# A recurrent layer's reciprocal on VectorE, replaced by an exponential on ScalarE and one Newton step

## The chip, the core and the metric

The kernel runs on one core of a Trainium2 chip. TensorE (PE) does the matrix products, VectorE (DVE) and ScalarE (ACT) the elementwise work, GpSimd (POOL) elementwise work and indirect loads, and SyncE (SP) issues most loads. The engines run side by side and wait for one another by semaphores. The metric is the device time of one execution in microseconds (us), the median of several runs.

## What is computed

One layer over 128 context and 512 latent tokens of width 1024, all in fp32. After a modulated norm come products with `w_in`, a bidirectional gated linear recurrence (the place of this change), a pooling branch, a merge, an output projection, and an expert mixer that takes more than two thirds of the time. The recurrence, cut to what matters:

```
def rglru_dir(x, wa, ba, wx, bx, lam, h0, reverse):
    r = jax.nn.sigmoid(blockdiag(xf, wa, ba))
    i = jax.nn.sigmoid(blockdiag(xf, wx, bx))
    log_a = RG_C * r * jax.nn.log_sigmoid(lam)            # RG_C = 8
    a = jnp.exp(log_a)
    bterm = jnp.sqrt(-jnp.expm1(2.0 * log_a)) * (i * xf)
    h = linear_scan(a, bterm, h0f)                        # h[t] = a[t] h[t-1] + bterm[t]

# mixer
hf, sf = rglru_dir(xr, ..., h0f, False)
hb, sb = rglru_dir(xr, ..., h0b, True)
branch_a = ((hf + hb) * jax.nn.gelu(yr)) @ w_up_rnn
```

The kernel avoids exp and expm1. With s = softplus(-lambda) and T = tanh(4 s r), the identities a = 2/(1+T) - 1 and sqrt(1 - a^2) = 2 sqrt(T)/(1+T) give both terms from one tanh, one sqrt and one reciprocal q = 1/(1+T).

## The kernel before

Activations lie transposed: 128 channels on the partitions, 640 tokens along the free dimension. A row block of 128 channels is a round; the recurrence has eight, m = 0 to 7, and each has two directions d = 0, 1. With a few columns of gap the two token groups make 644 columns.

Every 128x1024 weight block is split into a high and a low part, so that each fp32 product runs as three passes. ACT writes the high part `wHi` (`split`) once the product two places earlier is done, POOL writes the low part `wLo` by a subtraction that reads two tensors (`low_of`, L393), PE multiplies (`product`, L457), and ACT takes the result out of PSUM. The two PSUM and weight buffers alternate, so ACT must have taken out product g before PE may start g + 2.

The order on each engine is the order in which the program is written. `beside(m)` lists which products PE does in round m: xr(m+2), yr(m+1), gb(m+1) and upp(m) in rounds 1 to 5, only yr7 and gb7 in round 6, only upp6 and upp7 in round 7. Then follow the products ga2 to ga5. PE also does two small groups of gate products a round (`gates`, L543).

In round m, ACT does in this order: `sigs(m, 0)`, two sigmoids of the gate products of direction 0 (once `dir_done` says that DVE has finished direction 0 of round m - 1); the first product of `beside(m)`; `sigs(m, 1)`; Tanh for both directions (in place in `gr`); Sqrt for both (into `gs`, which signals `gates_act`); the other products' splits and evictions. All ACT instructions carry line 678. An `ACT_TABLE_LOAD` stands wherever the next function isn't in the loaded table: before Sqrt, before Gelu, and before the next Sigmoid.

In round m, DVE does: the convolution of the next round (`conv`, L1101 and L1103), one product of the pooling branch (`pooled_gate`, L1144), `direction(m, 0)`, `direction(m, 1)`, then the sum of both directions (L1155) and the product with gelu (L1158), which signals `a_ready`. `direction` is L1117 to L1136: 1 + T, the reciprocal (L1118), a = 2q - 1, i times x, the forcing term, and two scans into `hdir[d]`. `ch.step` is an instruction followed by DVE's own wait for its end; `ch.link` is one without that wait.

After round 7, ACT waits for the eighth `a_ready`, writes `aHi` (8 instructions), then splits the weights of ga5; POOL writes their low part, and only then can PE go on with ga5 and the products after it.

Of the kernel before, what the change touches and what calls it, by code (L numbers as in the profile page):

```python
# [49 lines left out]
def beside(m):  # L50

    if m == 0:
        return [("xr", 2), ("ga", 0), ("ga", 1), ("upp", 0)]
    if m < 6:
        return [("xr", m + 2), ("yr", m + 1), ("gb", m + 1), ("upp", m)]
    return [("yr", 7), ("gb", 7)] if m == 6 else [("upp", 6), ("upp", 7)]
# [87 lines left out]
def build(nc, xT, posT, cT, vecs_d, iota_d, invc_d, gw_d, pw_d, keys_d, wblk, ublk, u_tab, v_tab, ident_d, iota128_d, gel_d, gate_d, yT, st_out):  # L144
    f32, f32r, u32 = mybir.dt.float32, mybir.dt.float32r, mybir.dt.uint32
    ALU, ACT, AX = mybir.AluOpType, mybir.ActivationFunctionType, mybir.AxisListType
# [4 lines left out]
    def sb(name, shape, dt=f32):  # L151
        g = nc.sbuf_tensor(name, shape, dt)
        t = g.__enter__()
        keep.append(g)
        return t
# [5 lines left out]
    def sem(name):  # L161
        return nc.semaphore(name).__enter__()
# [19 lines left out]
    stfin = sb("stfin", [128, 2, KC])  # L182
    sp = sb("sp", [128, 16])
    sp4 = sb("sp4", [128, 16])
    spt = sb("spt", [128, 4, 16])
    halves_mark = len(keep)

# [29 lines left out]
    gr = [sb(f"gr{d}", [128, 2, WH]) for d in range(2)]  # L217
    gi = [sb(f"gi{d}", [128, 2, WH]) for d in range(2)]
    gs = [sb(f"gs{d}", [128, 2, WH]) for d in range(2)]
    gq = sb("gq", [128, W])  # L220
    hdir = [sb(f"hdir{d}", [128, W]) for d in range(2)]
# [47 lines left out]
             "head_done scm_ready exp_ready tr_done htok_ready e_ready row_free act_ready gel_ready acc_ready "  # L269
             "accT_done x3_ready y_ready y_st st_st st_ready dve_c act_c mod_ready pool_held dve_held "  # L270
             "w_hi act_held eg_ready gel_free bank_free gmm_done oh_ready sm_ready tr2_done wf_ready "
             "whi_ready wlo_ready hi_first crow_mm crow_ready crow_tr mod_read").split()
    gel_st = [sem(f"gel_st{j}") for j in range(2)]
    gate_st = [sem(f"gate_st{j}") for j in range(2)]
    gs_ld = [sem(f"gs_ld{j}") for j in range(4)]
    s = {n: sem(n) for n in names}
# [399 lines left out]
    def _(act):  # L676
        def actf(out, in_, f, **kw):
            return nc.scalar.activation(out, in_, f, **kw)  # L678
# [135 lines left out]
        def out_of(name, m):  # L814
            {"xr": xr_out, "yr": yr_out, "gb": gb_out, "ga": ga_out, "upp": upp_out}[name](m)

        def sigs(m, d):
            act.wait_ge(s["gates_done"], 2 * m + d + 1)
            if m >= 1:
                act.wait_ge(s["dir_done"], 2 * (m - 1) + d + 1)  # L820
            actf(gr[d][:, :, :], P[2][:, :, 0:WH], ACT.Sigmoid, bias=col(V_BA + d * 8 + m)).then_inc(s["act_c"], 1)
            actf(gi[d][:, :, :], P[3][:, :, 0:WH], ACT.Sigmoid, bias=col(V_BX + d * 8 + m)).then_inc(s["sig_done"], 1)
# [17 lines left out]
        for m in range(KC):  # L840
            sigs(m, 0)
            around = beside(m)
            out_of(*around[0])
            sigs(m, 1)
            act.wait_ge(s["act_c"], 1 + 4 * m + 2)
            for d in range(2):

                actf(gr[d][:, :, :], gr[d][:, :, :], ACT.Tanh, scale=sp4[:, d * 8 + m:d * 8 + m + 1]
                     ).then_inc(s["act_c"], 1)
            act.wait_ge(s["act_c"], 1 + 4 * m + 4)  # L850
            for d in range(2):
                actf(gs[d][:, :, :], gr[d][:, :, :], ACT.Sqrt).then_inc(s["gates_act"], 1)
            for name, b in around[1:]:
                out_of(name, b)
# [124 lines left out]
    def _(dve):  # L979
        V = nc.vector  # L980
        ch = Chain(dve, s["dve_c"], s["dve_held"])
# [60 lines left out]
        ch.step(V.tensor_tensor(e_, e_, z_, ALU.mult))  # L1042
        ch.step(V.tensor_scalar(z_, lam, -1.0, 0.0, ALU.mult, ALU.max))
        ch.step(V.scalar_tensor_tensor(out=sp[:, :], in0=e_, scalar=2.0, in1=z_, op0=ALU.mult, op1=ALU.add))
        V.tensor_scalar(sp4[:, :], sp[:, :], 4.0, None, ALU.mult).then_inc(s["sp_ready"], 1)
        V.tensor_tensor(pbias[:, :], vecs[:, V_PB:V_PB + 4], vecs[:, V_PS:V_PS + 4], ALU.mult)
        V.memset(px[:, :], 0.0).then_inc(s["xpp_ready"], 1)
# [61 lines left out]
        def flat(t3):  # L1109
            return t3[:, :, :].rearrange("p h n -> p (h n)")  # L1110

        def direction(m, d):
            r, i_, t_ = flat(gr[d]), flat(gi[d]), flat(gs[d])
            dve.wait_ge(s["gates_act"], 2 * m + d + 1)
            dve.wait_ge(s["conv_done"], m + 1)

            ch.step(V.tensor_scalar(gq[:, :], r, 1.0, None, ALU.add))  # L1117
            ch.step(V.reciprocal(gq[:, :], gq[:, :]))  # L1118
            ch.link(V.tensor_scalar(r, gq[:, :], 2.0, -1.0, ALU.mult, ALU.add))
            ch.link(V.tensor_tensor(i_, i_, xc[:, m % 2, :], ALU.mult))  # L1120
            ch.step(V.scalar_tensor_tensor(out=t_, in0=t_, scalar=2.0, in1=gq[:, :], op0=ALU.mult, op1=ALU.mult))
            ch.step(V.tensor_tensor(t_, t_, i_, ALU.mult))
            h = hdir[d]
            for g, (c0, c1) in enumerate(((0, TA), (TA + GAP, TA + GAP + TB))):
                init = 0.0 if g == 0 else vecs[:, V_ST + d * 8 + m:V_ST + d * 8 + m + 1]
                if d == 0:
                    o_, a_, b_ = h[:, c0:c1], r[:, c0:c1], t_[:, c0:c1]
                elif c0 == 0:
                    o_, a_, b_ = h[:, c1 - 1::-1], r[:, c1 - 1::-1], t_[:, c1 - 1::-1]
                else:  # L1130
                    o_, a_, b_ = h[:, c1 - 1:c0 - 1:-1], r[:, c1 - 1:c0 - 1:-1], t_[:, c1 - 1:c0 - 1:-1]
                last = V.tensor_tensor_scan(out=o_, data0=a_, data1=b_, initial=init, op0=ALU.mult, op1=ALU.add)
            last.then_inc(s["dir_done"], 1)
            dve.wait_ge(s["dir_done"], 2 * m + d + 1)
            e = TA - 1 if d == 0 else 0
            ins = V.tensor_copy(stfin[:, d, m:m + 1], h[:, e:e + 1])  # L1136
            if m == KC - 1 and d == 1:
                ins.then_inc(s["st_ready"], 1)
# [8 lines left out]
        for m in range(KC):  # L1147
            if m + 1 < KC:
                conv(m + 1)
            if 1 <= m < 7:  # L1150
                pooled_gate(m - 1)
            for d in range(2):
                direction(m, d)
            for (c0, c1, o) in ((0, TA, 0), (TA, T, GAP)):
                last = V.tensor_tensor(hs[:, m, c0:c1], hdir[0][:, c0 + o:c1 + o], hdir[1][:, c0 + o:c1 + o], ALU.add)  # L1155
            ch.step(last)
            evicted(dve, "yr", m)
            V.tensor_tensor(hs[:, m, :], hs[:, m, :], gy[:, m % 2, :], ALU.mult).then_inc(s["a_ready"], 1)  # L1158
# [28 lines left out]
        for m in range(KC):  # L1187
            pr = G["wo", m] % 2
            multiplied(dve, "wo", m)
            for (c0, c1, g) in ((0, TA, 0), (TA, HALF, 1), (HALF, T, 1)):  # L1190
                h = c0 // HALF
                last = V.scalar_tensor_tensor(out=x[:, m, c0:c1], in0=P[pr][:, h, c0 - h * HALF:c1 - h * HALF],
                                              scalar=mod[:, 16 + m, g:g + 1], in1=x[:, m, c0:c1],
                                              op0=ALU.mult, op1=ALU.add)
# [78 lines left out]
        for h in range(HEADS):  # L1273
            dve.wait_ge(s["S_ready"], 2 * h + 2)
            for t in range(NT):
                search((h, t), before)
                before = (h, t)
                if t == 0 and h > 0:
# [10 lines left out]
                               op0=ALU.mult, op1=ALU.add).then_inc(s["e_ready"], 1)  # L1289
# [89 lines left out]
        for k in range(KC):  # L1379
            last = V.scalar_tensor_tensor(out=x[:, k, TA:T], in0=P[k // 2][:, k % 2, :], scalar=mod[:, 40 + k, 1:2],  # L1380
                                          in1=x[:, k, TA:T], op0=ALU.mult, op1=ALU.add)
        last.then_inc(s["x3_ready"], 1)
        dve.wait_ge(s["accT_done"], 1)
        for k in range(KC):
            last = V.scalar_tensor_tensor(out=x[:, k, 0:TA], in0=P[0][:, k // 4, (k % 4) * 128:(k % 4 + 1) * 128],
                                          scalar=mod[:, 40 + k, 0:1], in1=x[:, k, 0:TA], op0=ALU.mult, op1=ALU.add)
        last.then_inc(s["x3_ready"], 1)
        inv_rms(2)
        with dve.Fori(0, KC) as k:
            V.scalar_tensor_tensor(out=hs[:, ds(k, 1), :].rearrange("p a n -> p (a n)"),  # L1390
                                   in0=x[:, ds(k, 1), :].rearrange("p a n -> p (a n)"),
                                   scalar=vecs[:, ds(k + V_FG, 1)], in1=rstd[:, :],
                                   op0=ALU.mult, op1=ALU.mult).then_inc(s["y_ready"], 1)
# [83 lines left out]
```

## Time and profile before

| | us |
|---|---|
| median of 3 runs | 2393.9 |
| lowest and highest | 2392.54, 2401.06 |
| the profiled execution | 2405.23 |
| its span in the trace | 2403.4 |
| mean granted TensorE clock | 0.967 |

Shares of the span, by engine: PE 95%, weight load 81%, DVE 70%, POOL 41%, ACT 34%. The recurrence's eight rounds lie between 156 and 397 us of the span. The chain of work that ended last is, by line, PE for 74% of the span and DVE for 6%; the reciprocal's line holds 1% of it.

To read the rows further down: a row of the timeline or of the chain has the start in us from the span's start, the duration in us, the engine and line, the operation, what is written and read, and in brackets the idle time of the engine before it and what ended that. A group with "x3" is three instructions. A row of one line gives the smallest, median and largest duration in ns. A row of the windows gives, for a stretch of time, the busy us of each engine (and its instructions), then the granted PE clock (1.00 is the full one), the DMA share and GB/s.

### The profile page before, as it was taken

How to read it: one execution, taken by the hardware profiler on the slowest of the kernel's cores; microseconds unless marked ns; L12 is line 12 of the kernel's file. 1: busy time of each engine (PE TensorE's matmuls, PEld its weight loads, DVE VectorE, ACT ScalarE, POOL GpSimd, SP SyncE). 2: the span in 40 equal slices, each digit the busy share in tenths (PEclk: the TensorE clock that was granted, in tenths of full speed). 3: DMA queues.
4: the chain of work that ended last, by engine and by line, in shares of the span. 5: the costliest groups of instructions: out<-in, count | busy, mean ns of one | idle time of the engine just before them, and what ended most of it. 6: DMA issues, size and time to landing. Idle time of an engine off the chain costs nothing.

```text
span 2403.4 us, 36139 instructions
## 1 busy us (share of the span) xinstructions
PE 2281.8 (95%) x11708; PEld 1947.9 (81%) x11708; DVE 1691.7 (70%) x3334; ACT 817.3 (34%) x1034; POOL 980.9 (41%) x578
## 2 busy tenths in 40 slices
PE   6799997999999999998999999998999999999995
PEld 2789987999999888786888888886888888888883
DVE  2549996131499999101888998997777777777775
ACT  1445553111323222222544444442222222222221
POOL 0223322222132444443222222225667666676671
PEclk9899998989799999999999999998999999999997
DMA  6412223333422444444688888877888888888881
GB/s 247 177 49 66 62 62 112 117 112 117 123 62 79 138 143 140 137 142 146 218 300 302 308 311 301 313 245 234 271 268 268 271 270 268 268 273 268 267 252 70
DMA packets 232787, 467.29 MB, mean 194 GB/s; under 512 B 115344, under 2 KB 115728, under 8 KB 231056
## 3 DMA queue, kind: packets, MB, share of 16 engines
q1 hardware_dynamic: 176416, 270.82, 36.6%
q0 software_dynamic: 36864, 134.23, 16.1%
q10 hardware_dynamic: 19440, 61.35, 6.4%
q8 instruction: 40, 0.66, 0.1%
q14 instruction: 27, 0.22, 0.0%
HBM read 402.37 MB, written 63.97 MB: 194 GB/s over the span
## 4 chain that ended last, share of the span: by engine, by line
PE 74%; issue 9%; DVE 6%; DMA 5%; POOL 3%; ACT 2%; DVEq 1%; ACTq 0%; SPq 0%; POOLq 0%
PE P L653 30%; PE P L457 19%; PE P L619 15%; POOL wLo L399 3%; PE P L642 3%; DMA rows<-in_u_tab,Eg 3%; PE P L479 3%; PE P L466 1%; PE P L543 1%; DMA gel_scratch<-gel 1%; DMA raw<-in_wblk 1%; PE P L499 1%; DVE ohA L1323 1%; DVE gq L1118 1%; DVE rows L1304 1%
## 5 line engine op out<-in xcount | busy, mean ns | idle before, releaser
L678 ACT ACTIVATE wHi<-raw 128x1024 fp32r<-128x1024 f32 x330 | 346.2, 1049 | 1354.2 <-PE P L653 509.6
L399 POOL TENSOR_TENSOR wLo<-raw,wHi 128x1024 fp32r<-128x1024 f32 x192 | 466.5, 2430 | 417.1 <-ACT wHi L678 416.9
L1366 DVE TENSOR_TENSOR wfLo<-wf,wfHi 128x512 fp32r<-128x512 f32 x128 | 313.8, 2452 | 165.4 <-ACT wfHi L678 165.4
L653 PE MATMUL P<-wfHi,wHi 128*128 128x512 f32 x1024 | 409.7, 400 | 10.2 <-DVE wfLo L1366 10.2
L619 PE MATMUL P<-hHi,wHi 128*128 128x512 f32 x1024 | 411.2, 402 | 3.7 <-DVE wLo L1311 3.2
L619 PE MATMUL P<-hHi,wLo 128*128 128x512 f32 x1024 | 406.3, 397 | 0.0
L653 PE MATMUL P<-wfHi,wLo 128*128 128x512 f32 x1024 | 404.4, 395 | 0.0
L619 PE MATMUL P<-hLo,wHi 128*128 128x512 f32 x1024 | 403.7, 394 | 0.0
L653 PE MATMUL P<-wfLo,wHi 128*128 128x512 f32 x1024 | 402.4, 393 | 0.0
L393 POOL TENSOR_TENSOR wLo<-raw,wHi 128x1024 fp32r<-128x1024 f32 (+1 forms) x76 | 182.6, 2404 | 502.4 <-ACT wHi L678 502.3
L418 POOL DMA_INDIRECT rows<-in_u_tab,Eg x128 | 134.6, 1052 | 357.4 <-DVE rows L1304 336.0
L457 PE MATMUL P<-hHi,wHi 128*128 128x320 f32 x960 | 233.3, 325 | 28.3 <-DVE hLo L986 12.7
L653 PEld LDWEIGHTS P<-wfHi,wHi 128*128 128x128 f32 x1024 | 192.9, 188 | 54.7 <-issue 10.4
L653 PEld LDWEIGHTS P<-wfHi,wLo 128*128 128x128 f32 x1024 | 192.8, 188 | 50.3
L619 PEld LDWEIGHTS P<-hHi,wHi 128*128 128x128 f32 x1024 | 193.3, 189 | 47.4 <-issue 4.5
L619 PEld LDWEIGHTS P<-hHi,wLo 128*128 128x128 f32 x1024 | 192.6, 188 | 46.9
L653 PEld LDWEIGHTS P<-wfLo,wHi 128*128 128x128 f32 x1024 | 192.8, 188 | 46.0
L619 PEld LDWEIGHTS P<-hLo,wHi 128*128 128x128 f32 x1024 | 193.1, 189 | 44.8
L457 PE MATMUL P<-hLo,wHi 128*128 128x320 f32 x960 | 223.7, 315 | 0.0
L457 PE MATMUL P<-hHi,wLo 128*128 128x320 f32 x960 | 222.7, 314 | 0.0
L457 PEld LDWEIGHTS P<-hHi,wHi 128*128 128x128 f32 x960 | 165.9, 194 | 33.7 <-issue 12.5
L1323 DVE TENSOR_SCALAR ohA<-iota,keysel,SC 128x128 f32<-128x128 f32 x512 | 178.2, 349 | 0.0
(172 smaller groups left out, 3264.2 us busy)
## 6 DMA issues: line engine op xcount, KB each, us to landing
raw<-in_ublk SPq DMA_DIRECT2D x128, 512.0 KB, 3.7
raw<-in_v_tab SPq DMA_DIRECT2D x128, 512.0 KB, 3.8
raw<-in_wblk SPq DMA_DIRECT2D x116, 512.0 KB, 3.7
gel_scratch<-gel ACTq DMA_DIRECT2D x128, 256.0 KB, 2.0
gsr<-gel_scratch SPq DMA_DIRECT2D x128, 256.0 KB, 6.2
gate_scratch<-stage ACTq DMA_DIRECT2D x6, 4096.0 KB, 17.0
gsr<-gate_scratch SPq DMA_DIRECT2D x128, 192.0 KB, 5.2
x<-in_xT SPq DMA_DIRECT2D x1, 2560.0 KB, 12.3
```

Of the source, the lines that this page charges most:

```text
L393: pool.tensor_tensor(wLo[:, g % 2, 0:kk], raw[:, r, 0:kk], wHi[:, g % 2, 0:kk].bitcast(f32), ALU.subtract).then_inc(raw_used[r], 1)
L399: pool.tensor_tensor(wLo[:, j % 2, :], raw[:, j, :], wHi[:, j % 2, :].bitcast(f32), ALU.subtract).then_inc(raw_used[j], 1)
L418: pool.indirect_dma_start(out=rows[:, j % UR, :], out_offset=None, in_=tab, in_offset=bass.IndirectOffsetOnAxis(ap=Eg[:, g, j:j + 1], axis ...
L457: last = nc.tensor.matmul(P[g % 2][:, h, 0:HALF], w_[:, g % 2, k * 128:(k + 1) * 128], cols(x_, k, h), start=(st and a == 0 and b == 0), s ...
L466: last = nc.tensor.matmul(P[2][:, h, 0:HALF], ones[:, :], sq[:, k % 2, h * HALF:(h + 1) * HALF], start=(k == 0), stop=(k == KC - 1))
L479: last = nc.tensor.matmul(P[3][:, MODB(m), MODC + m * 2:MODC + m * 2 + 2], raw[:, n % RAW, k * 128:(k + 1) * 128], cvec[:, 2 * k:2 * k + 2 ...
L619: last = nc.tensor.matmul(P[0][:, j % 2, :], w_[:, j % 2, k * 128:(k + 1) * 128], x_[:, k, TA:T], start=(k == 0 and a == 0 and b == 0), st ...
L642: last = nc.tensor.matmul(P[1][:, q, n * 128:(n + 1) * 128], ohB[:, q, n, :], ohA[:, q, n, :], start=True, stop=True)
L653: last = nc.tensor.matmul(P[k // 2][:, k % 2, :], w_[:, j % 2, k * 128:(k + 1) * 128], x_[:, j % 2, :], start=(first and a == 0 and b == 0 ...
L678: return nc.scalar.activation(out, in_, f, **kw)
L1323: last = V.tensor_scalar(ohA[:, q, n, :], iota128[:, :], keysel[:, 0:1, ds(c, 1)].rearrange("p a n -> p (a n)"), SC[:, ds(c, 1)], ALU.is_e ...
L1366: V.tensor_tensor(wfLo[:, j % 2, :], wf[:, j % 2, :], wfHi[:, j % 2, :].bitcast(f32), ALU.subtract).then_inc(s["wlo_ready"], 1)
```

## The change

The reciprocal q = 1/(1+T) goes. Since (1 + exp(-8 s r)) / 2 is the same number, ACT now computes exp(-8 s r) for both directions into `hdir[d]` (free at that time, since the scans write it later), from the r that Tanh then overwrites. DVE forms q0 from it and refines it by one Newton step. ACT has a new wait ahead of the exponentials: `a_ready` of the round before, since DVE still reads `hdir` until then. The Tanh pair waits for the end of both exponentials, `exp_done`. A vector `sp8` of scales is computed once.

```
@@ sp8 = sb("sp8", [128, 16]) is allocated; semaphore exp_done is added @@
             sigs(m, 1)
             act.wait_ge(s["act_c"], 1 + 4 * m + 2)
+            if m:
+                act.wait_ge(s["a_ready"], m)
+            for d in range(2):
+                actf(hdir[d][:, :], gr[d][:, :, :].rearrange("p h n -> p (h n)"), ACT.Exp,
+                     scale=sp8[:, d * 8 + m:d * 8 + m + 1]).then_inc(s["exp_done"], 1)
+            act.wait_ge(s["exp_done"], 2 * m + 2)
             for d in range(2):
                 actf(gr[d][:, :, :], gr[d][:, :, :], ACT.Tanh, scale=sp4[:, d * 8 + m:d * 8 + m + 1]
...
+        V.tensor_scalar(sp8[:, :], sp[:, :], -8.0, None, ALU.mult)
         V.tensor_scalar(sp4[:, :], sp[:, :], 4.0, None, ALU.mult).then_inc(s["sp_ready"], 1)
...
-            ch.step(V.tensor_scalar(gq[:, :], r, 1.0, None, ALU.add))
-            ch.step(V.reciprocal(gq[:, :], gq[:, :]))
-            ch.link(V.tensor_scalar(r, gq[:, :], 2.0, -1.0, ALU.mult, ALU.add))
+            ch.step(V.tensor_scalar(gq[:, :], hdir[d][:, :], 0.5, 0.5, ALU.mult, ALU.add))
+            ch.step(V.scalar_tensor_tensor(out=r, in0=r, scalar=1.0, in1=gq[:, :], op0=ALU.add, op1=ALU.mult))
+            ch.step(V.scalar_tensor_tensor(out=gq[:, :], in0=r, scalar=-2.0, in1=gq[:, :], op0=ALU.add, op1=ALU.mult))
+            ch.link(V.tensor_scalar(r, gq[:, :], -2.0, -1.0, ALU.mult, ALU.add))
             ch.link(V.tensor_tensor(i_, i_, xc[:, m % 2, :], ALU.mult))
-            ch.step(V.scalar_tensor_tensor(out=t_, in0=t_, scalar=2.0, in1=gq[:, :], op0=ALU.mult, op1=ALU.mult))
+            ch.step(V.scalar_tensor_tensor(out=t_, in0=t_, scalar=-2.0, in1=gq[:, :], op0=ALU.mult, op1=ALU.mult))
```

What stands on ACT in a round doesn't show in the diff alone. This is round 7 in the program before, from the sigmoids of direction 1 (into `gr` and `gi`) to the square roots (into `gs`):

```order
210 L678 ACTIVATE gr<-P,vecs 128x644 [waits dir_done,gates_done]
211 L678 ACTIVATE gi<-P,vecs 128x644
212 L678 ACTIVATE gr<-gr,sp 128x644 [waits act_c]
213 L678 ACTIVATE gr<-gr,sp 128x644
214 L678 ACT_TABLE_LOAD
215 L678 ACTIVATE gs<-gr 128x644 [waits act_c]
216 L678 ACTIVATE gs<-gr 128x644
```

The same stretch in the changed program:

```order
231 L679 ACTIVATE gr<-P,vecs 128x644 [waits dir_done,gates_done]
232 L679 ACTIVATE gi<-P,vecs 128x644
233 L679 ACT_TABLE_LOAD [waits a_ready]
234 L679 ACTIVATE hdir<-gr,sp 128x644 [waits act_c]
235 L679 ACTIVATE hdir<-gr,sp 128x644
236 L679 ACTIVATE gr<-gr,sp 128x644 [waits exp_done]
237 L679 ACTIVATE gr<-gr,sp 128x644
238 L679 ACT_TABLE_LOAD
239 L679 ACTIVATE gs<-gr 128x644 [waits act_c]
240 L679 ACTIVATE gs<-gr 128x644
```

A table load and two exponentials (`hdir<-gr,sp`) now stand between the sigmoids and the Tanh pair, with the wait for `a_ready` ahead of the load. Tanh follows Exp without a load of its own. Every round has this; no other instruction changes its place.

## Rows read from the trace of the kernel before

**Rows 1.** The page's first part: busy us, share of span, instructions of PE.

```profile
PE 2281.8 (95%) x11708; PEld 1947.9 (81%) x11708; DVE 1691.7 (70%) x3334; ACT 817.3 (34%) x1034; POOL 980.9 (41%) x578
```

**Rows 2.** Windows; columns: PE, weight load, DVE, ACT, POOL, clock, DMA, GB/s.

```profile
230.00:260.00 30.00, 30.00 (x193) 28.69 (x192) 28.95 (x27) 17.19 (x23) 9.67 (x5) 1.00 0.19 62
380.00:410.00 30.00, 19.00 (x132) 18.92 (x131) 23.89 (x29) 8.53 (x13) 7.90 (x3) 0.79 0.50 185
```

**Rows 3.** The chain that ended last, in order of time: start, us, what.

```profile
303.91 2.17 PE P L543 x8
...
332.89 2.17 PE P L543 x8
...
397.73 4.48 ACT aHi L678 x7
402.21 0.96 ACT wHi L678
403.23 4.41 POOL wLo L393
407.69 8.69 PE P L457 x48
```

**Rows 4.** Single lines of DVE: durations in ns, smallest, median, largest.

```profile
L1118 DVE RECIPROCAL gq<-gq x16: 4177/4178/4179, 176.0 to 386.5; 128x644 f32<-128x644 f32 x16
```

```profile
L1103 DVE SCALAR_TENSOR_TENSOR xc<-xrp,vecs,xc x24: 887/890/2923, 151.3 to 346.0; 128x644 f32<-128x644 f32 x24
```

**Rows 5.** Timeline of DVE, rounds 5 to 7.

```profile
320.34 0.50 DVE L1117 TENSOR_SCALAR gq<-gr 128x644 f32<-128x644 f32 x1 [0.56 <-ACT gs L678]
...
334.42 2.45 DVE L1119 TENSOR_SCALAR gr<-gq 128x644 f32<-128x644 f32 x1
...
341.87 0.83 DVE L1158 TENSOR_TENSOR hs<-hs,gy 128x640 f32<-128x640 f32 x1
...
351.17 0.50 DVE L1117 TENSOR_SCALAR gq<-gr 128x644 f32<-128x644 f32 x1 [3.55 <-ACT gs L678]
351.70 4.18 DVE L1118 RECIPROCAL gq<-gq 128x644 f32<-128x644 f32 x1
...
357.07 0.82 DVE L1121 SCALAR_TENSOR_TENSOR gs<-gs,gq 128x644 f32<-128x644 f32 x1
...
360.50 0.49 DVE L1117 TENSOR_SCALAR gq<-gr 128x644 f32<-128x644 f32 x1
...
370.74 0.82 DVE L1158 TENSOR_TENSOR hs<-hs,gy 128x640 f32<-128x640 f32 x1
374.82 0.50 DVE L1117 TENSOR_SCALAR gq<-gr 128x644 f32<-128x644 f32 x1 [3.26 <-ACT gs L678]
...
379.57 1.96 DVE L1119 TENSOR_SCALAR gr<-gq 128x644 f32<-128x644 f32 x1
...
396.23 0.82 DVE L1158 TENSOR_TENSOR hs<-hs,gy 128x640 f32<-128x640 f32 x1
```

**Rows 6.** Timeline of POOL, rounds 5 to 7.

```profile
323.14 1.29 POOL L393 TENSOR_TENSOR wLo<-raw,wHi 128x512 fp32r<-128x512 f32 x1 [5.70 <-ACT wHi L678]
...
334.12 2.39 POOL L393 TENSOR_TENSOR wLo<-raw,wHi 128x1024 fp32r<-128x1024 f32 x1 [1.11 <-ACT wHi L678]
...
362.99 2.34 POOL L393 TENSOR_TENSOR wLo<-raw,wHi 128x1024 fp32r<-128x1024 f32 x1 [9.35 <-ACT wHi L678]
376.45 4.73 POOL L393 TENSOR_TENSOR wLo<-raw,wHi 128x1024 fp32r<-128x1024 f32 x2 [11.12 <-ACT wHi L678]
```

**Rows 7.** Timeline of ACT, rounds 5 to 7.

```profile
300.49 1.06 ACT L678 ACTIVATE wHi<-raw 128x1024 fp32r<-128x1024 f32 x1 [4.39 <-PE P L457]
...
342.84 1.28 ACT L678 ACT_TABLE_LOAD   x1
...
370.50 0.79 ACT L678 ACTIVATE gi<-P,vecs 128x644 f32<-128x644 f32 x1
371.19 1.55 ACT L678 ACTIVATE gr<-gr,sp 128x644 f32<-128x644 f32 x2
372.75 1.28 ACT L678 ACT_TABLE_LOAD   x1
```

More of the change, by code:

```diff
@@ L184, in build @@
     sp4 = sb("sp4", [128, 16])
+    sp8 = sb("sp8", [128, 16])
     spt = sb("spt", [128, 4, 16])
@@ L271, in build @@
              "w_hi act_held eg_ready gel_free bank_free gmm_done oh_ready sm_ready tr2_done wf_ready "
-             "whi_ready wlo_ready hi_first crow_mm crow_ready crow_tr mod_read").split()
+             "whi_ready wlo_ready exp_done hi_first crow_mm crow_ready crow_tr mod_read").split()
     gel_st = [sem(f"gel_st{j}") for j in range(2)]
```

## The prediction

> **What bounds the kernel now.** I read the page's engine shares first: PE is busy for 95% of the span [rows 1], so only what makes PE wait can matter. Then the windows over the recurrence: in 230 to 260 us PE is busy for all 30.00 us, and DVE for 28.95 [rows 2]. The chain in order of time confirms that the rounds run at PE's pace: the gate products of two successive rounds start at 303.91 and 332.89, so a round is 28.98 us [rows 3]. DVE is nearly as full, but the chain doesn't run through it there. From round 6 on PE has few products left and the chain changes engines: in 380 to 410 us PE works only 19.00 of 30 us, at a granted clock of 0.79 [rows 2]. There the end of DVE's round 7 (396.23 + 0.82 = 397.05 us, [rows 5]) releases ACT's `aHi`, then a `wHi`, then POOL's `wLo`, and PE goes on at 407.69 [rows 3]. Everything later hangs on that instant, and nothing in it is changed. So the question is: when does the eighth `a_ready` come, 397.05 us before, and do rounds 1 to 5 stay at PE's pace?
>
> **What goes on DVE.** 16 reciprocals of 4.18 us [rows 4], each with 0.03 us until the next instruction (351.17 + 0.50 to 351.70, [rows 5]): 4.21 us. In comes, per direction, two operations of the form of L1121, 0.82 us plus 0.03 [rows 5]: 1.70 us. The two scalar operations around them stay, only their numbers and inputs change. So a direction falls by 2.5 us, from 9.33 (351.17 to 360.50, [rows 5]) to 6.83, and DVE has 16 x 2.5 = 40 us less work. In rounds 0 to 5 that is worth nothing, since PE sets the pace; what can shorten the end are the directions of rounds 6 and 7.
>
> **What comes on ACT.** No Exp is in these rows; the nearest row is the Tanh pair, same shape and same kind of scale: 1.55 us [rows 7]. Its bounds are that pair's cost and, from below, half of it should the instructions overlap entirely; I take 1.55, since it is the same engine over the same 644 columns. The order of the changed program has one table load more a round, 1.28 us [rows 7]. It starts when the second sigmoid is done (370.50 + 0.79 = 371.29, whereas Tanh started at 371.19): 0.1 us. With 0.05 us for the wait on `exp_done`, Tanh comes 0.1 + 1.28 + 1.55 + 0.05 = 3.0 us later in every round, and so does the DVE work that waits for it.
> The load's price by the row: Tanh runs from 371.19 for 1.55, the load starts at 372.75, at once, and takes 1.28. The Trainium skill ("ScalarE: Activation LUTs", What ACT_TABLE_LOAD costs) gives about 2.66 us for every switch, a drain of about 1380 ns included. The trace does not agree that a drain comes on top, so I leave it out; what it would do stands among the rivals.
>
> **The new wait.** ACT's load now waits for `a_ready` of the round before. Behind it are Exp, Tanh, Sqrt, the split for upp, the evictions of yr and gb and two more splits; PE waits for those evictions and, through POOL, for those splits. In rounds 1 to 5 they have cover: ACT is idle for 4.39 us before its `wHi` at 300.49 [rows 7], and 3.0 us later they still fit, with 1.4 us over. In rounds 6 and 7 they have none.
>
> **What the reciprocal covered.** POOL writes four `wLo` a round, three of about 2.4 us and one of 1.29 [rows 6]. The reciprocal isn't disturbed by them: 4177 to 4179 ns in all 16 [rows 4]. Other DVE operations are: L1119 takes 2.45 us at 334.42 beside POOL's 334.12, and 0.50 elsewhere, so it lost 1.95; L1103 takes up to 2923 ns against 890, so 2.03 [rows 4 to 6]. A short `wLo` should then cost 1.29 - (2.40 - 2.03) = 0.92. The new operations read two tensors, as L1103 does, so the `wLo` that lay under a reciprocal now hit. Bounds for one hit: 0 (if this form with a constant scalar is exempt) and the whole `wLo`, 2.4 or 1.29. I take 2.03 and 0.92, the measured ones.
> "SBUF — State Buffer" of the Trainium skill (SBUF: two separate sides) says that the ports shared by DVE and GpSimd are an exclusive lock, also for a DVE operation with two SBUF inputs against a GpSimd operation that reads SBUF. By that rule the exempt case is excluded; L1103's 2923 ns agrees with it, no row shows L1121's form beside POOL.
>
> **The sum, step by step.**
> 1. Round 5. Before: 320.34 to 342.70, 22.35 us, 1.95 of it a hit. New start 320.34 + 3.0 = 323.34. Length 22.35 - 1.95 - 5.0 = 15.4, plus hits of 0.92 + 2.03 + 2.03 from the three `wLo` in it, plus about 1.0 from one that starts near the end (at 343, for upp6): `a_ready` at 344.7, 2.0 later.
> 2. ACT's table load for Gelu at 342.84 [rows 7] has to wait for exactly that count: it moves to 344.7, 1.8 later. With it move the sigmoids of (6,1), and then come the 3.0: direction (6,0) starts at 351.17 + 4.8 = 356.0.
> 3. Direction (6,0) has the short `wLo` of upp7 in it, 0.92: (6,1) starts at 356.0 + 6.83 + 0.92 = 363.7, against 360.50. The split of ga2 waits for the sigmoids behind (6,0), so POOL's 362.99 [rows 6] moves along and falls into (6,1): 2.03. Before, 360.50 to 371.56 (end of L1158) were 11.06; now 11.06 - 2.5 + 2.03 = 10.6: `a_ready` at 374.3, 2.8 later.
> 4. Load 1.28, Exp 1.55, waits 0.1: Tanh at 377.25. From Tanh to DVE's start it was 374.82 - 371.19 = 3.63: (7,0) starts at 380.9, 6.1 later.
> 5. From there to the end it was 397.05 - 374.82 = 22.23, with 1.96 - 0.50 = 1.46 of a hit (L1119 at 379.57). New: 22.23 - 1.46 - 5.0 = 15.8, plus 2 x 2.03 for the two `wLo` of 376.45 that move along: 19.8. End: 400.7.
> That is 3.7 us later than 397.05. The rest of the chain is unchanged and shifts with it. PE would be idle for about 15 instead of 11 us before 407.69; the clock there is down already. `sp8` is one operation of 16 columns in a stretch where DVE has waits: nothing.
> The profiled execution's own 2405.23 us (span 2403.4) would become 2408.9. It lies 11.3 us above the median of the runs; the sum moves both alike: 2393.9 + 3.7 = 2397.6.
>
> **Rivals.**
> A. The new operations don't collide with POOL. Then round 5 ends before 342.7, (6,0) starts at 354.2, `a_ready` comes 13.66 + 1.74 later at 369.6, Tanh at 372.5, (7,0) at 376.2, the end at 392.0: 5.0 us earlier, 2388.9. For it: no row shows the form beside POOL. Against: the TENSOR_SCALAR and L1103 rows.
> B. The round becomes a loop through the new wait, longer than PE's. From `a_ready` to the next round's DVE start are 2.9 (load, Exp, wait) + 3.63 = 6.5 us; from there to `a_ready` 15.4 plus hits. Without hits 21.9 us; with four hits at the measured price, 3 x 2.03 + 0.92 = 7.0, it is 28.9, and PE's round is 28.98. That is the point from which it decides. I hold the rounds for covered because one of the four starts about when the convolution does, where DVE has some 2 us of room beside ACT's 6.5; so 26.9. If each hit costs the whole `wLo` and all four count, 3 x 2.4 + 1.29 = 8.5, the round is 30.4: 1.4 us more in each of rounds 1 to 6, so 8.6, and 3.7 at the end: 12.3 us, 2406.2. This is slower, and by just over 0.5%.
> C. The added table load costs more than its 1.28 us, say a second 1.28: 7.0 + 21.9 + 1.3 = 30.2 a round, 1.2 us x 6 = 7.3, and 2 x 1.28 + 3.7 at the end: 13.6, 2407.5. The row of the load at 372.75 speaks against it. That is the switch of the Trainium skill's page named above, which would make it 1.38 instead.
> D. DVE's saved time comes out whole, because the rounds hang on DVE after all (28.95 busy of 30): 16 x 2.5 = 40 us, 2354. PE's 30.00 of 30 speaks against it.
>
> **How the numbers follow.** The forecast gets 0.56, A 0.20, B 0.15, C 0.05, D 0.04. Faster by over 0.5% (12 us, about what a measurement of this kernel can tell from no change): D, 0.04. Slower by over 0.5%: B and C are at that edge; 0.18 with a little of the forecast's own spread. Within: 0.78. The range goes from A, 2388.9, to B, 2406.2, and a little further on both sides, since the three runs before lie 8.5 us apart: 2387 to 2408.
>
> **What would show it.** Right: no reciprocal, 16 directions of about 6.8 us where no `wLo` falls; one load more a round on ACT, at 1.28 us; gate products of successive rounds still 28.98 us apart up to round 6, PE busy for 30 of 30; operations of L1126 to L1133 with a largest duration near 2.8 us; first DVE work of round 7 near 381 and PE's ga5 near 411 us. Wrong: all those operations at 0.82 (A), rounds of over 29.5 us with PE idle before upp (B), a gap beside the loads (C), or a round much shorter than 28.98 (D).

## The result and the profile after

The changed kernel takes 2408.18 us (median of 20 runs, 2399.23 to 2416.59), the kernel before 2397.72 us over the 20 runs that were set against it. The ratio is 1.0038, 95% interval 1.0028 to 1.0049: slower by 9 us, 7 to 12. Against that stood a forecast of 3.7 us more. The stated range, 2387 to 2408 us, ends just where 2408.18 lies; counted from the forecast's own starting value, 2393.9 x 1.0038 = 2403.0 is inside it.

The profiled execution of the changed kernel happens to be one of its fastest, 2401.24 us with a span of 2399.4. Spans of single executions say little here; what holds is the position of events inside the recurrence, and the counts in long stretches.

The chain that ended last, changed kernel, in order of time (start, us, what):

```profile
303.12 2.17 PE P L544 x8
...
312.32 2.18 PE P L544 x8
316.03 1.28 ACT L679
317.33 1.57 ACT hdir L679 x2
318.92 1.56 ACT gr L679 x2
...
406.40 4.41 POOL wLo L394
410.86 9.40 PE P L458 x48
```

Up to round 5 PE still sets the pace: the gate products of rounds 4 and 5 start at 274.15 and 303.12, 28.97 us apart, against 28.98 in [rows 3]. Then the chain leaves PE one round earlier than before, through the new exponentials. ga5 starts at 410.86 instead of 407.69, in both kernels 10.64 us after the end of the eighth `a_ready`.

DVE's timeline in rounds 4 to 7 of the changed kernel (compare [rows 5]; the first row is the fifth `a_ready`):

```profile
313.19 0.83 DVE L1167 TENSOR_TENSOR hs<-hs,gy 128x640 f32<-128x640 f32 x1
...
330.38 2.43 DVE L1125 TENSOR_SCALAR gq<-hdir 128x644 f32<-128x644 f32 x1
...
333.71 2.92 DVE L1127 SCALAR_TENSOR_TENSOR gq<-gr,gq 128x644 f32<-128x644 f32 x1
...
342.15 1.89 DVE L1167 TENSOR_TENSOR hs<-hs,gy 128x640 f32<-128x640 f32 x1
...
355.46 0.50 DVE L1125 TENSOR_SCALAR gq<-hdir 128x644 f32<-128x644 f32 x1 [7.38 <-ACT gs L679]
...
356.86 1.77 DVE L1127 SCALAR_TENSOR_TENSOR gq<-gr,gq 128x644 f32<-128x644 f32 x1
...
363.25 0.50 DVE L1125 TENSOR_SCALAR gq<-hdir 128x644 f32<-128x644 f32 x1
...
366.65 2.97 DVE L1130 SCALAR_TENSOR_TENSOR gs<-gs,gq 128x644 f32<-128x644 f32 x1
...
373.15 0.82 DVE L1167 TENSOR_TENSOR hs<-hs,gy 128x640 f32<-128x640 f32 x1
380.58 0.50 DVE L1125 TENSOR_SCALAR gq<-hdir 128x644 f32<-128x644 f32 x1 [6.61 <-ACT gs L679]
...
382.84 2.52 DVE L1128 TENSOR_SCALAR gr<-gq 128x644 f32<-128x644 f32 x1
385.29 3.00 DVE L1129 TENSOR_TENSOR gi<-gi,xc 128x644 f32<-128x644 f32 x1
...
399.39 0.83 DVE L1167 TENSOR_TENSOR hs<-hs,gy 128x640 f32<-128x640 f32 x1
```

The fifth `a_ready` ends at 314.02, and the load that needs it starts at 316.03, right behind a sigmoid: 2.0 us to spare. From round 6 on there is nothing to spare.

The undisturbed direction is (7,1): 391.64 to 398.47, 6.83 us. All the others of rounds 5 to 7 hold an operation of 1.8 to 3.0 us, where a `wLo` of POOL hits. And ahead of (6,0) and (7,0) DVE waits for ACT, 7.38 and 6.61 us instead of 3.55 and 3.26 [rows 5].

What ACT does in that time, rounds 6 and 7 of the changed kernel (compare [rows 7]):

```profile
344.12 1.28 ACT L679 ACT_TABLE_LOAD   x1 [2.10 <-DVE hs L1167]
...
372.92 0.79 ACT L679 ACTIVATE gi<-P,vecs 128x644 f32<-128x644 f32 x1
374.05 1.28 ACT L679 ACT_TABLE_LOAD   x1 [0.34 <-DVE hs L1167]
375.35 1.56 ACT L679 ACTIVATE hdir<-gr,sp 128x644 f32<-128x644 f32 x2
376.94 1.56 ACT L679 ACTIVATE gr<-gr,sp 128x644 f32<-128x644 f32 x2
378.52 1.28 ACT L679 ACT_TABLE_LOAD   x1
```

The load at 344.12 waits for the sixth `a_ready`, as step 2 of the sum said; the one at 374.05 waits 0.34 us for the seventh. POOL's low parts in the same rounds start at these times (compare [rows 6]):

```profile
356.66 1.28 POOL L394 TENSOR_TENSOR wLo<-raw,wHi 128x512 fp32r<-128x512 f32 x1 [13.30 <-ACT wHi L679]
366.01 2.93 POOL L394 TENSOR_TENSOR wLo<-raw,wHi 128x1024 fp32r<-128x1024 f32 x1 [8.07 <-ACT wHi L679]
382.21 5.39 POOL L394 TENSOR_TENSOR wLo<-raw,wHi 128x1024 fp32r<-128x1024 f32 x2 [13.27 <-ACT wHi L679]
```

Each lies beside one of the long DVE operations above. So inside the recurrence nearly everything went as forecast: the eighth `a_ready` at 400.22, 3.2 us after 397.05, and 4.0 if one allows for this execution being 0.8 us ahead at round 5 (303.12 against 303.91). PE's waits moved, however. Ahead of ga5 it waits 6.57 us, where the forecast said about 15 and the kernel before has 11.00; ahead of the gate products of round 7 it waits 8.84 instead of 5.02, and 2.42 more ahead of a product at 385.06. Together that is 17.8 us instead of 16.0.

What the forecast lacks is 5 us that this stretch doesn't hold.

The windows show where they are. Two stretches that the change doesn't touch, the first in the expert scores, the second in the expert values (L619 and L653; PE busy, then its instructions in brackets), first in the kernel before:

```profile
860.00:1100.00 240.00, 239.59 (x1027) 192.48 (x1026) 106.78 (x343) 65.02 (x85) 107.04 (x43) 1.00 0.44 139
1700.00:2300.00 600.00, 600.00 (x2573) 482.67 (x2572) 465.16 (x429) 169.86 (x216) 417.05 (x241) 1.00 0.87 269
```

then in the changed kernel:

```profile
860.00:1100.00 240.00, 239.66 (x1024) 192.39 (x1023) 105.25 (x335) 65.88 (x86) 104.75 (x43) 1.00 0.43 140
1700.00:2300.00 600.00, 600.00 (x2563) 482.36 (x2562) 463.00 (x426) 169.07 (x214) 415.49 (x241) 1.00 0.86 269
```

At full granted clock and with PE busy throughout, the changed kernel does 1024 matmuls where there were 1027, and 2563 where there were 2573. A matmul takes 234.4 instead of 233.7 ns in the scores and 234.1 instead of 233.2 in the values; over 3072 matmuls in each stage that is 2.1 + 2.8 = 4.9 us. The length of the values' stage shows it too. From its first matmul to its last it takes 717.9 to 719.2 us in the six traces without the 64-byte tile `sp8`, and 721.5 to 722.3 in the eight traces with it (the kernels of the next section included). The length of the scores' stage, 861 to 871 us with the work between, varies too much to show it.

### The profile page after: what moved, and what is told of

Its sections match the earlier page's. It is cut to its first block, busy times and chain, and to the rows that moved or that the text cites. A ratio compares the mean times of both kernels' runs of the same rounds, so it can differ in the third digit from the quotient of the medians.

```text
span 2399.4 us, 36187 instructions
## 1 busy us (share of the span) xinstructions
PE 2281.2 (95%) x11708; PEld 1945.3 (81%) x11708; DVE 1675.9 (70%) x3351; ACT 839.9 (35%) x1058; POOL 983.0 (41%) x578
## 4 chain that ended last, share of the span: by engine, by line
PE 73%; issue 9%; DVE 6%; DMA 5%; POOL 3%; ACT 3%; DVEq 0%; ACTq 0%; SPq 0%; POOLq 0%
PE P L654 30%; PE P L458 17%; PE P L620 16%; POOL wLo L400 3%; PE P L643 3%; DMA gel_scratch<-gel 3%; PE P L480 2%; DMA rows<-in_u_tab,Eg 1%; PE P L467 1%; PE P L544 1%; PE P L500 1%; DMA raw<-in_wblk 1%; DVE ohA L1332 1%; DVE ohB L1330 1%; DVE rows L1313 1%
```

## The experiments

Twelve kernels ran, each beside the kernel before in five rounds, which gave 12 runs of most of them and 5 or 6 of e1, e2 and e11. The theories: **shift** (the end moves by exactly what the eighth `a_ready` moves), against **surcharge** (PE's longer waits in rounds 6 and 7 cost more later), and, once the windows were read, **placement** (the added tile makes later matmuls slower). In the table the shift is the end of the eighth `a_ready` less 397.05; "tile" is 4.9 where the kernel has the 64-byte tile `sp8`; "measured" is the ratio less one, times 2400.

| kernel | eighth a_ready | shift | shift + tile | ratio (95%) | measured, us |
|---|---|---|---|---|---|
| changed, 20 runs | 400.2 | +3.2 | +8.1 | 1.0038 (1.0028 to 1.0049) | +9.1 |
| e1 changed again | 400.2 | +3.1 | +8.0 | 1.0041 (1.0027 to 1.0055) | +9.8 |
| e2 ScalarE part | 425.9 | +28.8 | +33.7 | 1.0158 (1.0143 to 1.0174) | +37.9 |
| e3 VectorE part | 393.4 | -3.6 | +1.3 | 1.0003 (0.9990 to 1.0016) | +0.7 |
| e4 delay | 401.1 | +4.1 | +4.1 | 1.0002 (0.9989 to 1.0015) | +0.5 |
| e5 no added load | 396.4 | -0.6 | +4.3 | 1.0035 (1.0019 to 1.0050) | +8.4 |
| e6 no hits | 390.6 | -6.4 | -1.5 | 1.0007 (0.9987 to 1.0026) | +1.7 |
| e7 order, before | 395.5 | -1.6 | -1.6 | 1.0003 (0.9987 to 1.0018) | +0.7 |
| e8 order, changed | 386.9 | -10.1 | -5.2 | 0.9981 (0.9964 to 0.9998) | -4.6 |
| e9 tile alone | 397.2 | +0.2 | +5.1 | 1.0015 (0.9998 to 1.0032) | +3.6 |
| e10 changed, no tile | 400.1 | +3.1 | +3.1 | 1.0016 (1.0001 to 1.0031) | +3.8 |
| e11 order, no tile | 386.5 | -10.6 | -10.6 | 0.9940 (0.9921 to 0.9958) | -14.4 |
| e12 tile of 128 bytes | 397.3 | +0.2 | +0.2 | 0.9980 (0.9967 to 0.9992) | -4.8 |

**e1, the changed kernel again.** No edit.

> The changed kernel once more, beside the others. Shift theory (the end moves by exactly what the eighth a_ready moves, 3 to 4 us): 1.0013 to 1.0017 times the kernel before. Surcharge theory (the longer waits of PE in rounds 6 and 7 cost some 5 us more later, by a lower granted clock or late transfers): 1.003 to 1.0045. In the trace the eighth a_ready lies near 400 us under both; under the surcharge theory some later stage is longer than before by 3 us or more in this trace too.

1.0041, the eighth `a_ready` at 400.16. The excess over the shift came again: 6.7 us, where the interval allows 3.4 to 10. By the letter of the expectation the surcharge theory was the nearer one, but its cause (clock, transfers) isn't what this trace has: 1024 and 2563 matmuls in the two stretches again, at granted clock 1.00. Over all runs the mean granted clock is 0.9682 here and 0.9687 in the kernel before beside it. By the estimate made under e12 that is about 1 us.

**e2, ScalarE's part alone.** The DVE lines are those of before; Exp pair, load and wait stay.

```
-            ch.step(V.tensor_scalar(gq[:, :], hdir[d][:, :], 0.5, 0.5, ALU.mult, ALU.add))
...
+            ch.step(V.tensor_scalar(gq[:, :], r, 1.0, None, ALU.add))
+            ch.step(V.reciprocal(gq[:, :], gq[:, :]))
```

> ScalarE's part alone: Exp pair, table load, wait for a_ready; VectorE keeps the reciprocal and leaves the exponential unread. Computes the reference's result. Every round's VectorE work starts 3.0 us later with nothing given back: (6,0) near 357, (7,0) near 384, eighth a_ready near 406.3, so +9.2 us. A round's loop is 2.9 + 3.6 + 22.4 = 28.9 us, at the edge of TensorE's 28.98: if it exceeds it the rounds stretch and it is +12 us or more. If the ScalarE part did not matter: no change.

It is 38 us slower, far beyond the 9.2, and the other case named came true: the rounds stretch. The chain, from one exponential load to the next:

```profile
204.16 1.28 ACT L679
205.46 1.57 ACT hdir L679 x2
...
235.90 0.84 DVE hs L1166
236.81 1.28 ACT L679
...
266.73 0.84 DVE hs L1166
267.63 1.28 ACT L679
```

PE has left the chain. A load starts right behind DVE's `a_ready` operation, 32.65 and then 30.82 us apart, against PE's 28.98. And PE waits, in 160 to 450 us, for sigmoids, evictions and low parts that stand behind this on ACT:

```profile
PE P L544 <- ACT gi L679: 14.7, 2, 11.6
PE P L458 <- POOL wLo L394: 11.5, 2, 8.4
PE P L458 <- ACT gy L679: 10.3, 4, 3.4
```

So the loop of rival B exists. In the changed kernel the shorter directions keep it 2.0 us below PE's round (the fifth `a_ready` and the load behind it, above). The expected 28.9 us for e2's loop was too little, because it counted one hit a round. The round of the last load shown has three: a SCALAR_TENSOR_TENSOR of 3.03 us at 280.06, a scan of 2.52 instead of 0.42 at 283.99 and a TENSOR_SCALAR of 2.73 at 292.54.

**e3, VectorE's part alone.**

```
-            ch.step(V.tensor_scalar(gq[:, :], hdir[d][:, :], 0.5, 0.5, ALU.mult, ALU.add))
+            ch.step(V.tensor_scalar(gq[:, :], r, 0.5, 0.5, ALU.mult, ALU.add))
```

with the Exp pair and its waits left out.

> VectorE's part alone: the three new operations in place of the reciprocal, reading gr instead of an exponential; no Exp, no added load, no added wait. Leaves the exponential out, so the numbers of the recurrence are not the reference's. Forecast's mechanism: directions of 6.8 us plus hits of about 2.0 and 0.9 us; (6,0) still at 351, (7,0) near 372.8, eighth a_ready near 392.6, -4.4 us. If the whole VectorE saving were on the path: -40 us. If the new operations cost as much as the reciprocal once GpSimd hits them: 0.

The eighth `a_ready` came at 393.4 (392.6 expected). The whole VectorE saving of 40 us is worth 3.6 at this point. The total didn't fall by it (1.0003). With the tile's 4.9 us the sum is +1.3, inside the interval (-2.4 to 3.8); without it, -3.6 is not.

**e4, a delay.**

```
+            if m == 7:
+                for _ in range(4):
+                    ch.step(V.tensor_tensor(gq[:, :], gq[:, :], gq[:, :], ALU.mult))
```

in the kernel before, ahead of the last sum.

> The kernel before, with four extra VectorE operations (about 3.4 us together) ahead of the last sum of round 7. Nothing else changes. Shift theory: eighth a_ready +3.4 us and the total +3.4 us (1.0014). Surcharge theory by a longer idle stretch of TensorE before ga5: the total rises by clearly more, 6 us or more (1.0025 up).

`a_ready` moved by 4.1 us and the total by 0.5 (-2.6 to 3.6). This speaks against a surcharge from PE's longer idle stretch, and the shift itself lies just outside the interval. PE's wait ahead of ga5 did grow, from 11.00 to 14.41 us. So it is not shown that the end follows the eighth `a_ready` to the microsecond.

**e5, no added load.**

```
-                actf(hdir[d][:, :], gr[d][:, :, :].rearrange("p h n -> p (h n)"), ACT.Exp,
+                actf(hdir[d][:, :], gr[d][:, :, :].rearrange("p h n -> p (h n)"), ACT.Tanh,
```

> The changed kernel with Tanh in place of Exp in the added pair, so that no table load is added; the pair, its waits and VectorE's work stay. Its recurrence is not the reference's. By the price of the load as the row shows it (1.28 us a round, three rounds of it on the path): eighth a_ready about 3.9 us earlier than in the changed kernel, about equal to the kernel before (ratio 1.000 under the shift theory). If a load cost another 1.3 us, 7 to 8 us earlier.

The eighth `a_ready` is at 396.4, 3.8 us earlier: three loads of 1.28 us and nothing more. The total stayed at 1.0035; the sum with the tile is +4.3, just outside the interval (4.6 to 12.0). Its runs had a mean granted clock of 0.9675 against 0.9686 in the kernel before, by the estimate under e12 some 2 to 3 us; what lowered it isn't shown.

**e6, the hits taken away.**

```
+            if G["xr", 3] <= g <= G["ga", 4]:
+                kk = 16
```

in POOL's `low_of`.

> The changed kernel with GpSimd's low parts cut to 16 columns for the products from xr3 to ga4, so that they hardly meet VectorE; the products of these blocks are not the reference's. Rival A's time: no hits, eighth a_ready near 392 us, 5 us earlier than before and 8 to 9 earlier than the changed kernel. If the hits are not what the gain went to, it stays near 400.

The row of the second Newton operation, changed kernel first, then this one (busy us and mean ns of one, then idle before):

```profile
L1127 DVE SCALAR_TENSOR_TENSOR gq<-gr,gq 128x644 f32<-128x644 f32 x16 | 32.5, 2031 | 0.6
```

```profile
L1129 DVE SCALAR_TENSOR_TENSOR gq<-gr,gq 128x644 f32<-128x644 f32 x16 | 14.2, 890 | 0.6
```

2031 ns on the average against 890: this one line lost 18.3 us to POOL. The eighth `a_ready` is at 390.6, 9.6 us before that of the changed kernel. The six directions of rounds 5 to 7 gain 15 us by the arithmetic, so the hits are where most of the DVE gain in the last rounds went.

**e7, per-direction order in the kernel before.** In rounds 6 and 7 ACT does:

```
+            if m >= 6:
+                for d in range(2):
+                    sigs(m, d)
...
+                    actf(gr[d][:, :, :], gr[d][:, :, :], ACT.Tanh, ...)
...
+                    actf(gs[d][:, :, :], gr[d][:, :, :], ACT.Sqrt).then_inc(s["gates_act"], 1)
+                    if d == 0:
+                        out_of(*around[0])
```

> The kernel before, with ScalarE's Tanh and Sqrt done for each direction right behind its sigmoids in rounds 6 and 7 (one table load more a round, in idle time of ScalarE). Computes the reference's result. VectorE's waits of 3.55 and 3.26 us ahead of (6,0) and (7,0) should go: eighth a_ready near 390.2, -6.8 us, ratio 0.997. If these waits are covered by something else late: no change.

The waits are gone, but `a_ready` came only 1.6 us earlier, not 6.8. DVE's timeline:

```profile
346.91 0.49 DVE L1132 TENSOR_SCALAR gq<-gr 128x644 f32<-128x644 f32 x1
...
363.10 3.03 DVE L1136 SCALAR_TENSOR_TENSOR gs<-gs,gq 128x644 f32<-128x644 f32 x1
...
375.54 2.98 DVE L1135 TENSOR_TENSOR gi<-gi,xc 128x644 f32<-128x644 f32 x1
378.44 2.99 DVE L1136 SCALAR_TENSOR_TENSOR gs<-gs,gq 128x644 f32<-128x644 f32 x1
```

(6,0) starts with no idle time before it. But moved by a few us, the directions meet `wLo` outside their reciprocals: three operations of 3.0 us, and a TENSOR_SCALAR of 1.47 at 351.64, instead of one TENSOR_SCALAR of 1.96 [rows 5]. I had left the hits where they were. Total: no change.

**e8, the same order in the changed kernel**, with the exponentials of these rounds written over `xrp[:, d, 0:W]`, the convolution's input, by then used up.

> The changed kernel with the same order in rounds 6 and 7, and the exponentials of these rounds written over the convolution's spent input, so that they do not wait for a_ready. Computes the reference's result. VectorE's waits of 7.4 and 6.6 us ahead of (6,0) and (7,0) should go: eighth a_ready near 386, 14 us earlier than the changed kernel and 11 earlier than the kernel before, ratio near 0.9955 under the shift theory; 0.993 if the surcharge goes as well because TensorE no longer idles at gates (7,1).

The eighth `a_ready` is at 386.9 as expected, but the total fell by 4.6 us, not by 10. With the tile's 4.9 us the sum is -5.2, inside the interval (-8.6 to -0.5).

**e9, the tile alone**, in the kernel before:

```
+    sp8 = sb("sp8", [128, 16])
```

> The kernel before with nothing but the tile sp8 (64 bytes a partition) allocated, unread and unwritten, at the place where the change has it; every tile allocated behind it lies 64 bytes further on. Placement theory (the matmuls of the expert and value stages are slower by 0.3 to 0.4% in every kernel with that tile): 1024 instead of 1027 matmuls in 860 to 1100 us, 2563 instead of 2573 in 1700 to 2300 us, eighth a_ready unchanged near 397, total +5.2 us, 1.0022. Rival (the added instructions, their place in memory, or chance): 1027 and 2573 matmuls, 1.0000.

```profile
860.00:1100.00 240.00, 239.66 (x1023) 192.38 (x1023) 104.49 (x333) 66.42 (x86) 105.40 (x43) 1.00 0.43 140
1700.00:2300.00 600.00, 600.00 (x2563) 482.33 (x2562) 463.12 (x426) 169.07 (x214) 416.46 (x241) 1.00 0.87 269
```

An allocation that no instruction touches brings the counts of the changed kernel, to one matmul. So the slower matmuls are shown, and that the tile causes them. The time, 1.0015 (0.9998 to 1.0032), includes both +4.9 us and nothing. The three pairs with and without the tile all go the same way, by amounts that scatter: e9 against the kernel before 3.6 us, the changed kernel against e10 5.3, e8 against e11 9.8.

**e10, the changed kernel without the tile**: `sp8 = spt[:, 2, :]`, a quarter of `spt` that is otherwise unused.

> The changed kernel with the scales of the exponential kept in a spare quarter of spt, so that no tile is added and every other tile lies where it does in the kernel before. Computes the reference's result. Placement theory: eighth a_ready near 400.2 as in the changed kernel, 1027 and 2573 matmuls in the two stretches, total 3 to 4 us over the kernel before, 1.0013 to 1.0017. Rival: 1024 and 2563 matmuls and 1.004 as in the changed kernel.

```profile
860.00:1100.00 240.00, 239.58 (x1028) 192.41 (x1027) 109.66 (x359) 66.48 (x86) 106.47 (x43) 1.00 0.44 140
1700.00:2300.00 600.00, 600.00 (x2573) 482.67 (x2572) 464.80 (x428) 169.86 (x216) 417.18 (x242) 1.00 0.87 269
```

`a_ready` as in the changed kernel, counts as before (to one matmul), 1.0016: the 3 to 4 us of the shift are what is left: 3.8 us (0.2 to 7.4).

**e11, order of e8 without the tile.**

> The changed kernel in the per-direction order of rounds 6 and 7 and without the added tile. Computes the reference's result. Placement theory: eighth a_ready near 387, 2573 matmuls, so 10 us less than the kernel before, 0.9958. Rival: as with the tile, 0.998.

0.9940 (0.9921 to 0.9958): 14 us faster than the kernel before, and some 23 faster than the change as made (14.4 + 9.1; the two didn't run side by side). PE's waits in 335 to 515 us:

```profile
PE P L458 <- POOL wLo L394: 4.6, 2, 2.7
PE P L458 <- DVE hLo L1198: 4.6, 1, 4.6
PE P L544 <- ACT gi L679: 1.8, 1, 1.8
```

Before, it was 11.0 us ahead of ga5 and 5.0 ahead of the gate products of round 7. Expected were 10 us, at the upper edge of the interval (-19.0 to -10.1). The new order and the exponential's freedom from `a_ready` came together in e8 and e11; what each gives isn't separated.

**e12, a tile of 128 bytes** in the kernel before, otherwise as e9.

> As the tile alone, but 128 bytes. If the placement matters by whether addresses are off a 128-byte step, this is the kernel before again: 1027 and 2573 matmuls, 1.0000. If any shift costs, or a wider pattern decides: 1024 and 2563 or another number, about 1.002.

```profile
1700.00:2300.00 600.00, 600.00 (x2573) 483.05 (x2572) 463.84 (x430) 169.09 (x214) 416.50 (x243) 1.00 0.87 269
```

The counts are back at 1027 and 2573. The total is even 4.8 us below (1.9 to 7.9), though the instructions and `a_ready` are those of before. Its 12 runs had a mean granted clock of 0.9699, the 29 runs of the kernel before beside them 0.9685. Within those 29 runs, 0.001 more of that clock goes with about 2.2 us less (a straight line through them, so an estimate), which would be some 3 of the 4.8 us. Why the clock was higher with the same work is open. In e9 it was 0.9684, within 0.0001 of the kernel before.

Differences of this size between kernels should be taken as uncertain by some us more than the intervals say: four of the thirteen rows of the table (e2, e4, e5, e12) have their sum just or clearly outside their interval.

## Why the prediction was right or wrong, point by point

**What bounds the kernel** was right. PE kept the pace up to round 5, and the eighth `a_ready` released ga5: in the kernel before, the changed one, e4, e7, e9, e10 and e11 ga5 starts 10.6 us after it, wherever it lies between 386.5 and 401.2.

**DVE's arithmetic** was right: a direction of 6.83 us, read off (7,1).

**ACT's 3.0 us** were right: load 1.28, pair 1.56, small waits. They left the room forecast in rounds 1 to 5 (2.0 us between `a_ready` and the load, so a loop of 27.0 us, forecast 26.9). Gaps of 0.02 us beside the loads, and e5's 3.8 us for three loads, leave no room for a second price: rival C falls. So the 2.66 us for a switch that the Trainium skill gives ("ScalarE: Activation LUTs", What ACT_TABLE_LOAD costs) are not seen here; the load followed directly on the end of the last activation.

**The hits** were right in kind and about right in size: 1.78 instead of 0.83 for the short `wLo` (0.95, forecast 0.92), 2.97 instead of 0.82 for the long one (2.15, forecast 2.03). Rival A falls with them; e6 shows the time it would have given, 390.6 (I had 392.0). The exclusive use of the shared ports that "SBUF — State Buffer" of the Trainium skill describes (SBUF: two separate sides) agrees: here a SCALAR_TENSOR_TENSOR with two SBUF inputs and a constant is blocked, while the reciprocal, with one, was not.

**The sum** gave 2.0 us at the sixth `a_ready`, 2.8 at the seventh and 3.7 at the eighth. The trace has 1.3, 2.4 and 3.2, or 2.1, 3.2 and 4.0 from round 5's start on.

**Rival B**, the loop, did not decide, but it was no phantom: e2 is that loop. The upper end of the range came from B. That the measured time lies at or inside it is luck: B's 12.3 us did not occur, and what brought the time there was something that no rival named.

**What failed** is the last line of the sum, in two halves: that `sp8` costs "nothing", and that "the rest of the chain is unchanged and shifts with it". I priced the instruction and not the allocation. `sp8` is 64 bytes ahead of every tile allocated after it. Among these are `hHi`, `hLo`, `wfHi` and `wfLo`, the operands that the expert stages multiply with the weights; the weights `wHi` and `wLo` lie ahead of it and did not move. With that, the matmuls of the two expert stages are slower by 0.3 to 0.4%, 4.9 us. The shift at the eighth `a_ready` was about right, 3.2 to 4.0 against 3.7, and e10's +3.8 for the end agrees (0.2 to 7.4). The term for the rest of the chain was 4.9 us too small. Shift and tile make 8.1 of the 9.1 us. A smaller miss is PE's wait: the forecast put about 15 us ahead of ga5, and it was 6.6, because the gate products of round 7 came later as well. The predicted 2397.6 also started from a median of three runs, 2393.9, that 17 more runs moved to 2397.7.

**What stays open.** Which of the shifted tiles matters, and in what way the placement acts. Two shifts were tried, 64 bytes (slower) and 128 (not). The products of the recurrence, 320 columns instead of 512, did not slow down: rounds of 28.98 us before and 28.97 after. How much of a shift reaches the end isn't settled (e4), and the clock that goes with part of e12's 4.8 us has no cause.

## What to carry to other kernels

An instruction that is slow in itself can be cheap where another engine's work hides under it: before replacing it, look at what runs beside it and whether the replacement would be hit. A saving on an engine that others pace is worth only what the last rounds make of it. There the arithmetic alone moved the eighth `a_ready` by -3.6 us (e3) and the order of the feeding engine alone by -1.6 (e7); together, with the exponential freed of its wait, they moved it by -10.6 (e11). And a new tile is part of a change: put a small one into spare room, as e10 did (behind the large tiles was not tried), and count the matmuls of an untouched stretch to see whether they moved.

## What the runs showed of the hardware

- The start addresses of tiles matter to TensorE by a small, steady amount: with the tiles behind `sp4` moved by 64 bytes a 512-column fp32r matmul took 234.1 to 234.4 ns instead of 233.2 to 233.7 (e9), with 128 bytes it did not (e12), at the same granted clock of 1.00.
- Reciprocal of 128x644 takes 4.18 us on VectorE and isn't slowed by a GpSimd operation with two SBUF inputs: 4177 to 4179 ns in all 16, one of them over POOL's `wLo` of 352.37 to 353.64. TENSOR_SCALAR, TENSOR_TENSOR, SCALAR_TENSOR_TENSOR and scans were each seen held for nearly its whole length (1.9 to 2.2 of 2.4 us; in e2 a scan of 0.42 took 2.52).
